# Second attention's column norms: factors spread by products, or written to DRAM and read back to all partitions

## The chip, the core and the metric

The kernel runs on one core of a Trainium2 chip. The metric is the device time of one execution in microseconds (us); the time of a kernel is the median of its runs. A profile of one execution lies beside it, taken by the hardware profiler. Times inside it are counted from the start of its span.

The engines are TensorE (PE; its weight loads are listed as PEld), VectorE (DVE), ScalarE (ACT), GpSimd (POOL) and SyncE (SP). In this kernel SP issues all transfers between DRAM and the on-chip memory (SBUF). PE writes its results to eight banks of PSUM, which are named `ps`.

## The reference, cut to what matters

The whole program is two transformer blocks in sequence. The change lies in the second one, in its second attention (stick breaking, 8 heads of 128). Ahead of that attention the queries and the keys are normed, each head's column of 128 numbers by itself:

```python
def rmsnorm(x, gain):
    xf = x.astype(jnp.float32)
    y = xf * lax.rsqrt(jnp.mean(xf * xf, axis=-1, keepdims=True) + RMS_EPS)
    return (y * gain.astype(jnp.float32)).astype(x.dtype)
...
    qs = rmsnorm(heads(sq, SB_DH), sbq_gain)
    ks = rmsnorm(heads(sk, SB_DH), sbk_gain)
    o_sb = stick_breaking_attention(qs, ks, heads(sv, SB_DH)).astype(hn.dtype).reshape(B, T, SB_W)
```

There are 528 positions, 16 learned ones and 512 of the sequence. For a query of head h at position t the factor is one over the root of the mean of 128 squares plus a small number.

## The kernel before, in words

The kernel keeps activations transposed: features lie on the 128 partitions, positions along the free dimension. A tile of one head's queries is 128 x 512, of its keys 128 x 528. So a norm needs, for each position, a sum over partitions, and then the factor of that position on all 128 partitions.

The dense products take their weights from one stream in DRAM, in chunks of 512 KB. A chunk is loaded to `raw` (L259, on SP), split into a high and a low part by ACT (`split_hi`, L272) and DVE (`split_lo`, L279), and used by 8 groups of three matmuls (`three`, L294 to L296) for each range of columns. The split of a chunk is made three chunks ahead, and it is the work of the evacuation of the chunk that has just been multiplied.

A stage is a set of lanes that run `together` (L679): each lane gives each engine a generator which yields due times, and `weave` (L667) writes the instructions of one engine in the order of those due times. An engine runs its instructions strictly in that order, waits included. At the end of the stage all engines meet.

The stage of the change, from about 1632 to 1715 us, has four lanes:

- `SecondBranch` (L1734): eight chunks of the second branch product. PE multiplies `o_hi` and `o_lo` with a chunk into bank 6 or 7; DVE evacuates it with two instructions (L1766, L1768) into `merged`, then splits the low part of a later chunk (L279); SP loads the two tiles of `branch_in` that DVE needs (L1752) and stores `merged` to DRAM (`pre_spill`, L1756). A chunk's bank is free for the chunk after next when L1766 is done. Its due times run from 0 to 8, one unit for each chunk.
- The column norms, `NormCols` (L1050), of 16 tiles: 8 of keys (`sb_k`), then 8 of queries (`v_rows`). Due times are 0.6 to 8, with a step of 0.2 for spreading. They have two passes.
- `ValueRows` (L1697): eight times a load of a value tile (L1710), five transposing products on PE (L1722, L1723), and two copies on ACT, from 5 to 8. SP's loads of it stand in one queue with those of `SecondBranch`.
- `Lead` (L789): after everything else, PE multiplies the first chunk of the next stage, so that it has work while the other engines finish.

The first pass of `NormCols` loads a tile (L1079), squares it on ACT into one half of `sq` (L1088), and adds it up over partitions with a product on PE (L1101) which puts the sums of tile i on row i of a PSUM bank, columns 0 to 263 on rows 0 to 15 and the others on rows 32 to 47. When all 16 tiles are in, ACT takes the roots (L1091), DVE the reciprocals (L1120), and DVE multiplies with a constant by row (L1121). Then `rt`, 64 x 264, holds all factors, one row for each half of a tile.

The second pass spreads the factors and norms the tiles. For tile i, PE multiplies row i of `rt` with a broadcast column of the identity (L1111), for each half; each half is recorded as two matmuls. This puts the factor of each position on all partitions of a PSUM bank. Two pairs of banks, (2, 3) and (4, 5), take turns. DVE multiplies the tile with the spread factors and with the gain of its partition, in place, one instruction for each half (L1128). PE waits with tile i until tile i-2 is normed.

The due times put the second pass of this stage between 4.8 and 8. On DVE that gives this order: one norm, the evacuation of chunk 4, five norms, chunk 5, five norms, chunk 6, five norms, chunk 7. `NormCols` is used in two more stages, which the change leaves alone. POOL has no work in this stage.

```python
    def spread_time(self, i):
        n = len(self.tiles)
        return self.t1 - (n - i) * self.step
```

Of the kernel before, what the change touches and what calls it, by code (L numbers as in the profile page):

```python
# [20 lines left out]
F32 = mybir.dt.float32  # L21
F32R = mybir.dt.float32r
ACT = mybir.ActivationFunctionType
ALU = mybir.AluOpType
# [3 lines left out]
P = 128  # L28
# [6 lines left out]
HALF = T2 // 2  # L35
# [97 lines left out]
def param_array(v):  # L133
# [12 lines left out]
    def pairs(pe):  # L146
        return pe.reshape(CMP_J, P).T
# [90 lines left out]
class Chain:  # L238


    def __init__(self, sem):
        self.sem, self.count = sem, 0
# [69 lines left out]
def cst(K, name, rows=P):  # L312

    a, n = CONST_COLS[name]
    a1 = CONST_COLS["of block 1"][0]
    return K.const1[0:rows, a - a1:a - a1 + n] if a >= a1 else K.const[0:rows, a:a + n]


def par(K, name, rows=P):
    a, n = PARAM_COLS[name]  # L320
    return K.param[0:rows, a:a + n]
# [319 lines left out]
class Lane:  # L641
# [9 lines left out]
    def pe(self, pe):  # L651
        yield from ()
# [4 lines left out]
    def dve(self, dve):  # L657
        yield from ()

    def pool(self, pool):  # L660
        yield from ()
# [17 lines left out]
def together(K, *lanes):  # L679
    with K.nc.Block() as block:  # L680
        @block.sync
        def _(sp):
            weave(sp, [lane.sp for lane in lanes])

        @block.tensor
        def _(pe):
            weave(pe, [lane.pe for lane in lanes])

        @block.scalar
        def _(act):  # L690
            weave(act, [lane.act for lane in lanes])

        @block.vector
        def _(dve):
            weave(dve, [lane.dve for lane in lanes])

        @block.gpsimd
        def _(pool):
            weave(pool, [lane.pool for lane in lanes])
# [13 lines left out]
PRODUCT_SEMS = ("banks_free", "pieces")  # L713
# [333 lines left out]
NORM_COL_SEMS = tuple(f"tile_in_{i}" for i in range(16)) + ("n_squares", "n_sums", "n_roots", "n_factors", "n_spread", "n_normed")  # L1047


class NormCols(Lane):  # L1050
# [39 lines left out]
        act.wait_ge(z["n_sums"], n)  # L1090
        act.activation(self.rt[:], K.ps[0:64, 0, 0:HALF], ACT.Sqrt, bias=self.bias).then_inc(z["n_roots"], 1)  # L1091

    def pe(self, pe):
        K, z, n = self.K, self.z, len(self.tiles)
        for i, (x, _) in enumerate(self.tiles):
            yield self.square_time(i + 0.7)
            if i == 0 and self.free is not None:
                pe.wait_ge(*self.free)
            pe.wait_ge(z["n_squares"], i + 1)
            for h, (a, e) in enumerate(self.halves(x)):  # L1100
                mm = pe.matmul(K.ps[32 * h:32 * h + 32, 0, 0:e - a], cst(K, "pick")[:, 15 - i:47 - i], self.sq[:, i % 2, a:e],  # L1101
                               start=i == 0, stop=i == n - 1, skip_group_check=True)
            mm.then_inc(z["n_sums"], 1)
        for i, (x, _) in enumerate(self.tiles):
            yield self.spread_time(i)
            if i == 0:
                pe.wait_ge(z["n_factors"], 1)
            if i >= len(self.pairs):
                pe.wait_ge(z["n_normed"], i - len(self.pairs) + 1)
            for h, (a, e) in enumerate(self.halves(x)):  # L1110
                mm = pe.matmul(K.ps[:, self.pairs[i % len(self.pairs)] + h, 0:e - a],  # L1111
                               cst(K, "ident")[32 * h:32 * h + 32, 32 * h + i:32 * h + i + 1].broadcast_to([32, P]),
                               self.rt[32 * h:32 * h + 32, 0:e - a], start=True, stop=True)
            mm.then_inc(z["n_spread"], 1)

    def dve(self, dve):
        K, z, n = self.K, self.z, len(self.tiles)
        yield self.spread_time(0) - self.step
        dve.wait_ge(z["n_roots"], 1)
        K.dve_chain.link(dve, dve.reciprocal(self.rt[:], self.rt[:]))  # L1120
        dve.tensor_scalar(self.rt[:], self.rt[:], cst(K, self.scales, 64), None, ALU.mult).then_inc(z["n_factors"], 1)  # L1121
        for i, (x, gain) in enumerate(self.tiles):
            yield self.spread_time(i + 0.5)
            dve.wait_ge(z["n_spread"], i + 1)
            by = 1.0 if gain is None else gain
            b = self.pairs[i % len(self.pairs)]
            for h, (a, e) in enumerate(self.halves(x)):
                last = dve.scalar_tensor_tensor(x[:, a:e], K.ps[:, b + h, 0:e - a], by, x[:, a:e], ALU.mult, ALU.mult)  # L1128
            last.then_inc(z["n_normed"], 1)


ROW_SEMS = ("rows_in", "r_transposed", "r_act", "r_dve")
# [561 lines left out]
VALUE_SEMS = ("values_in_0", "values_in_1", "v_t", "v_out")  # L1694
# [1262 lines left out]
def named_sems(K, *groups):  # L2957
    names = [n for g in groups for n in g]
    return dict(zip(names, sems(K, *names)))


def block2(K, v):
# [3 lines left out]
    STORED = STORED_SEMS  # L2966
    taps = par(K, "conv2").rearrange("p (g f t) -> p g f t", g=2, t=4)
    with ExitStack() as c:
# [6 lines left out]
        with ExitStack() as c2:  # L2975
# [3 lines left out]
            with ExitStack() as c3:  # L2979
# [3 lines left out]
                z = named_sems(K, PRODUCT_SEMS, ("gate_free", "gate_pieces", "convolved", "silu", "tapped", "last_square"), FACTOR_SEMS, STORED, GATE_SEMS, NORM_COL_SEMS,  # L2983
                               ROW_SEMS)
# [12 lines left out]
            z = named_sems(K, PRODUCT_SEMS, STORED, DELTA_SEMS)  # L2997
# [3 lines left out]
        with ExitStack() as c2:  # L3001
            S.qk = scratch(K, c2, "qk_cols", [P, 8, T2])
            with ExitStack() as c3:
                ring = scratch(K, c3, "ring", [P, 3, T2])
                z = named_sems(K, PRODUCT_SEMS, STORED, OUT_SEMS, NORM_COL_SEMS)
# [7 lines left out]
            with ExitStack() as c3:  # L3013
                vT = scratch(K, c3, "v_cols", [P, 8, T2])
                ring = scratch(K, c3, "ring", [P, 3, T2])
                z = named_sems(K, PRODUCT_SEMS, STORED, ROW_SEMS)
# [4 lines left out]
            z = named_sems(K, PRODUCT_SEMS, STORED, DELTA_SEMS)  # L3021
# [3 lines left out]
        with ExitStack() as c2:  # L3025
            ring = scratch(K, c2, "ring", [P, 3, T2])
            z = named_sems(K, PRODUCT_SEMS, STORED, OUT_SEMS)
            together(K, DeltaOutput(K, S, o_hi, o_lo, D2["dz"], 8, z, c2, 0, 8),
                     Stored(K, [(8, XQ, D2["gdn"], 0, rs, (ACT.Tanh, 0.5))], ring, (6, 7), z, 0, 8, 1))
        qT = S.v.rearrange("p m j n -> p (m j n)").rearrange("p (h t) -> p h t", h=8)  # L3030
        with ExitStack() as c2:
            kT, v_rows = scratch(K, c2, "sb_k", [P, SB_H, T2]), scratch(K, c2, "sb_v", [P, 5, 1024])
            with ExitStack() as c3:
                z = named_sems(K, PRODUCT_SEMS, STORED, NORM_COL_SEMS, VALUE_SEMS, ("branch_in_0", "branch_in_1", "branch_taken"))
                dense = SecondBranch(K, o_hi, o_lo, D2["br0"], D2["gdn"], D2["pre"], c3, (6, 7), z, 0, 8)
                together(K, NormCols(K, [(kT[:, i], par(K, "sbk_gain")) for i in range(8)] + [(qT[:, i], par(K, "sbq_gain")) for i in range(8)],
                                     [(D2["sbk"], i) for i in range(8)] + [(D2["sbq"], i) for i in range(8)], None, 128 * EPS,
                                     "sb_scales", (2, 4), z, c3, 0.6, 8, 0.2),
                         ValueRows(K, v_rows, D2["sbv"], z, c3, 0, (z["n_roots"], 1), 5, 8),
                         dense, Lead(K, XQ, dense))  # L3040
            with ExitStack() as c3:
                ring = scratch(K, c3, "ring", [P, 2, SEQ])
                z = named_sems(K, PRODUCT_SEMS, STORED, STICK_SEMS)
                together(K, StickBreaking(K, qT, kT, v_rows, z, c3, 0, 8),
                         Stored(K, [(8, XQ, D2["gsb"], 0, rs, None)], ring, (6, 7), z, 0, 8, 1))
# [6 lines left out]
def core_setup(nc, ctx, v, n_stream):  # L3052
    K = Core()
    K.live, K.cleared, K.uid = [], [], 0
    K.nc, K.stage, K.at, K.stream, K.n_stream = nc, 0, 0, v["stream"], n_stream

    def sb(name, shape, dt=F32):
        return ctx.enter_context(nc.sbuf_tensor(name, shape, dt))

    K.ps = ctx.enter_context(nc.psum_tensor("ps", [P, 8, 512], F32))  # L3060
    K.raw = sb("raw", [P, RAW, 1024])
    K.whi, K.wlo = sb("whi", [P, HL, 1024], F32R), sb("wlo", [P, HL, 1024], F32R)
    K.h = sb("h_sb", [P, KT, SEQ])
    K.const, K.param = sb("const_sb", [P, CONST_COLS["of block 1"][0]]), sb("param_sb", [P, PARAM_N])
    K.nx_hi, K.nx_lo = sb("nx_hi", [P, KT, T2], F32R), sb("nx_lo", [P, KT, T2], F32R)
    K.spill = {n: nc.dram_tensor(f"{n}_spill", (P, w, T2), F32, kind="Internal").ap() for n, w in (
        ("qk0", 8), ("v0", 8), ("qk1", 8), ("v1", 8), ("dz", 16), ("sbq", 8), ("sbk", 8), ("sbv", 8), ("br0", 8), ("gdn", 8),
        ("pre", 8), ("gsb", 8))}
    K.s_out = ctx.enter_context(nc.semaphore("out_written"))
    K.t_ss, K.t_rs = sb("t_ss", [P, TT]), sb("t_rs", [P, TT])  # L3070
    K.s_raw = [ctx.enter_context(nc.semaphore(f"raw_in_{i}")) for i in range(RAW)]
    K.s_hi, K.s_lo, K.s_used = [ctx.enter_context(nc.semaphore(n)) for n in ("hi_made", "lo_made", "chunk_used")]
    K.act_chain = Chain(ctx.enter_context(nc.semaphore("act_step")))
    K.dve_chain = Chain(ctx.enter_context(nc.semaphore("dve_step")))
    K.pool_chain = Chain(ctx.enter_context(nc.semaphore("pool_step")))
    return K
# [39 lines left out]
```

## Time and profile before

| | us |
|---|---|
| median of 3 runs (2331.86 to 2341.15) | 2336.89 |
| the profiled execution's own time | 2338.18 |
| its span | 2336.4 |
| busy PE | 2225.7 |
| busy DVE | 1125.4 |
| busy ACT | 813.3 |
| busy POOL | 64.6 |

The profiled execution is 1.3 us above the median, and 1.8 us of its time lie outside the span. The profile's busy time of an engine is an average over stages with different limits; the stage of the change is a small part of the span, and which engine bounds it has to be read from that stretch. The chain of work that ended last can be followed back only through the last 18% of the span, so it says nothing of this stage.

### The profile page before, as it was taken

Reading aid. Unit: us, or ns where it says so; the run is one execution under the profiler, and the core shown is the slowest. Engines: PE = TensorE matmul, PEld = TensorE weight load, DVE = VectorE, ACT = ScalarE, POOL = GpSimd, SP = SyncE. Lnnn points to the kernel's source line nnn. Section 1 sums busy time; section 2 is a strip of 40 time slices with the busy share of each in tenths; the row PEclk is TensorE's granted clock in tenths of the full one; section 3 lists DMA queues with packets and bytes.
Section 4 is the critical chain, followed back from the end, with each engine's and each line's share of the span. In section 5 each row is a group of like instructions: output and inputs, shape, how many; then the busy total and the mean of one; then the engine's idle time right before and its main releaser. Section 6 shows DMA issues by size and latency. Waiting matters only on the chain. (4 is left out here: it accounts for less than half of the span.)

```text
span 2336.4 us, 32788 instructions
## 1 busy us (share of the span) xinstructions
PE 2225.7 (95%) x13572; PEld 1706.8 (73%) x13572; DVE 1125.4 (48%) x1804; ACT 813.3 (35%) x1326; POOL 64.6 (3%) x88
## 2 busy tenths in 40 slices
PE   8999799999999899989998999998999999999999
PEld 7776457777778898976765788766565578888887
DVE  3465675666643366654434534345432245444422
ACT  3342554333332443332214222225355533322211
POOL 0000001000000000000000000000011101000000
PEclk9999799999999999999999999999999999999999
DMA  4124001222232243321114322114721132222222
GB/s 165 65 72 144 1 1 63 90 82 90 81 108 90 78 151 120 122 103 65 61 67 152 123 95 69 56 59 159 239 73 41 56 143 90 96 93 97 92 97 90
DMA packets 78595, 218.62 MB, mean 94 GB/s; under 512 B 8688, under 2 KB 13168, under 8 KB 78448
## 3 DMA queue, kind: packets, MB, share of 16 engines
q1 hardware_dynamic: 78448, 216.54, 26.7%
q8 instruction: 107, 1.75, 0.3%
q14 instruction: 40, 0.33, 0.0%
HBM read 185.70 MB, written 29.75 MB: 92 GB/s over the span
## 5 line engine op out<-in xcount | busy, mean ns | idle before, releaser
L294 PE MATMUL ps<-nx_hi,whi 128*128 128x264 f32 (+1 forms) x1504 | 543.0, 361 | 17.4 <-DVE nx_lo L383 9.9
L279 DVE TENSOR_TENSOR wlo<-raw,whi 128x1024 fp32r<-128x1024 f32 x282 | 346.5, 1229 | 393.4 <-ACT whi L272 392.9
L295 PE MATMUL ps<-nx_lo,whi 128*128 128x264 f32 (+1 forms) x1504 | 515.0, 342 | 0.0
L296 PE MATMUL ps<-nx_hi,wlo 128*128 128x264 f32 (+1 forms) x1504 | 514.7, 342 | 0.0
L272 ACT ACTIVATE whi<-raw 128x1024 fp32r<-128x1024 f32 x282 | 297.8, 1057 | 524.5 <-PE ps L296 422.7
L294 PEld LDWEIGHTS ps<-nx_hi,whi 128*128 128x128 f32 x1504 | 288.9, 192 | 82.4 <-issue 34.5
L296 PEld LDWEIGHTS ps<-nx_hi,wlo 128*128 128x128 f32 x1504 | 289.2, 192 | 32.8
L295 PEld LDWEIGHTS ps<-nx_lo,whi 128*128 128x128 f32 x1504 | 289.8, 193 | 29.3 <-issue 1.7
L294 PE MATMUL ps<-x_hi,whi 128*128 128x512 f32 x528 | 209.8, 397 | 14.8 <-DVE wlo L279 14.8
L296 PE MATMUL ps<-x_hi,wlo 128*128 128x512 f32 x528 | 209.8, 397 | 0.0
L295 PE MATMUL ps<-x_lo,whi 128*128 128x512 f32 x528 | 208.4, 395 | 0.0
L294 PEld LDWEIGHTS ps<-x_hi,whi 128*128 128x128 f32 x528 | 99.1, 188 | 45.5 <-DVE wlo L279 22.7
L295 PEld LDWEIGHTS ps<-x_lo,whi 128*128 128x128 f32 x528 | 99.2, 188 | 24.2
L296 PEld LDWEIGHTS ps<-x_hi,wlo 128*128 128x128 f32 x528 | 99.1, 188 | 23.1
L294 PE MATMUL ps<-act_hi,whi 128*128 128x512 f32 x288 | 113.3, 393 | 0.9 <-DVE wlo L279 0.9
L296 PE MATMUL ps<-act_hi,wlo 128*128 128x512 f32 x288 | 114.1, 396 | 0.0
L295 PE MATMUL ps<-act_lo,whi 128*128 128x512 f32 x288 | 114.0, 396 | 0.0
L294 PE MATMUL ps<-o_hi,whi 128*128 128x512 f32 x192 | 84.5, 440 | 8.7 <-DVE o_lo L1922 4.5
L858 DVE TENSOR_TENSOR ring<-ps,factor 128x512 f32<-128x512 f32 (+1 forms) x72 | 41.2, 572 | 82.8 <-PE ps L296 78.4
L295 PE MATMUL ps<-o_lo,whi 128*128 128x512 f32 x192 | 77.3, 402 | 0.0
L296 PE MATMUL ps<-o_hi,wlo 128*128 128x512 f32 x192 | 76.7, 399 | 0.0
L593 DVE TENSOR_TENSOR ps<-ps,factor 128x512 f32<-128x512 f32 x66 | 45.8, 693 | 49.7 <-PE ps L296 49.7
(454 smaller groups left out, 2906.9 us busy)
## 6 DMA issues: line engine op xcount, KB each, us to landing
raw<-stream_dram SPq DMA_DIRECT2D x285, 512.0 KB, 3.5
qk_spill<-ring SPq DMA_DIRECT2D x16, 264.0 KB, 2.2
qk_cols<-qk_spill SPq DMA_DIRECT2D x16, 264.0 KB, 4.0
v_spill<-ring SPq DMA_DIRECT2D x16, 264.0 KB, 2.1
v_cols<-v_spill SPq DMA_DIRECT2D x16, 264.0 KB, 4.2
dz_spill<-ring SPq DMA_DIRECT2D x16, 256.0 KB, 2.1
dz<-dz_spill SPq DMA_DIRECT2D x16, 256.0 KB, 5.1
sbk_spill<-ring SPq DMA_DIRECT2D x8, 264.0 KB, 2.1
```

The lines of the kernel that those rows point to most:

```text
L272: act.activation(K.whi[:, n % HL], K.raw[:, n % RAW], ACT.Copy).then_inc(K.s_hi, 1)
L279: dve.tensor_tensor(K.wlo[:, n % HL], K.raw[:, n % RAW], K.whi[:, n % HL].bitcast(F32), ALU.subtract).then_inc(K.s_lo, 1)
L294: pe.matmul(out, whi, xhi, start=start, stop=False, skip_group_check=skip)
L295: pe.matmul(out, whi, xlo, start=False, stop=False, skip_group_check=skip)
L296: return pe.matmul(out, wlo, xhi, start=False, stop=stop, skip_group_check=skip)
L593: dve.tensor_tensor(ps, ps, rs[:], ALU.mult).then_inc(z["scaled"], 1)
L858: dve.tensor_tensor(y, ps, by[:, a:e], ALU.mult).then_inc(self.free, 1)
```

## The change

The column norms of this stage become `NormColsByRow`. The first pass and the factors in `rt` stay. In the second pass PE has no work any more. POOL writes `rt` to a new DRAM tensor of 64 x 264, waits until it has landed, and then reads, for each half of each tile, the one row of factors into all 128 partitions of `sq`, whose two halves (free after the first pass) take turns. POOL waits with tile i until tile i-2 is normed. DVE norms a tile from `sq` in one instruction for its whole width instead of two. Due times on DVE are as before.

```diff
+class NormColsByRow(NormCols):
...
+    def pool(self, pool):
+        z = self.z
+        pool.wait_ge(z["n_factors"], 1)
+        pool.dma_start(self.factors, self.rt[:]).then_inc(z["factors_out"], 16)
+        pool.wait_ge(z["factors_out"], 16)
+        for i, (x, _) in enumerate(self.tiles):
+            if i >= 2:
+                pool.wait_ge(z["n_normed"], i - 1)
+            for h, (a, e) in enumerate(self.halves(x)):
+                pool.dma_start(self.sq[:, i % 2, a:e],
+                               self.factors[32 * h + i:32 * h + i + 1, 0:e - a].broadcast_to([P, e - a])).then_inc(z[f"spread_in_{i % 2}"], 16)
+        yield from ()
+
+    def pe(self, pe):
+        yield from self.sums(pe)
+
+    def dve(self, dve):
+        z = self.z
+        yield from self.roots(dve)
+        for i, (x, gain) in enumerate(self.tiles):
+            yield self.spread_time(i + 0.5)
+            dve.wait_ge(z[f"spread_in_{i % 2}"], 32 * (i // 2 + 1))
+            n = x.shape[1]
+            dve.scalar_tensor_tensor(x[:, 0:n], self.sq[:, i % 2, 0:n], 1.0 if gain is None else gain, x[:, 0:n],
+                                     ALU.mult, ALU.mult).then_inc(z["n_normed"], 1)
...
-                together(K, NormCols(K, [(kT[:, i], par(K, "sbk_gain")) for i in range(8)] + [(qT[:, i], par(K, "sbq_gain")) for i in range(8)],
+                together(K, NormColsByRow(K, K.factors, [(kT[:, i], par(K, "sbk_gain")) for i in range(8)] + [(qT[:, i], par(K, "sbq_gain")) for i in range(8)],
...
+    K.factors = nc.dram_tensor("factors_spill", (64, HALF), F32, kind="Internal").ap()
```

`sums` and `roots` are the first halves of `pe` and `dve` of `NormCols`, cut out as functions without a change to what they issue.

## Rows read from the trace of the kernel before

**Rows 1.** The page, part 1: busy time, share of the span, instructions of each engine.
```profile
PE 2225.7 (95%) x13572; PEld 1706.8 (73%) x13572; DVE 1125.4 (48%) x1804; ACT 813.3 (35%) x1326; POOL 64.6 (3%) x88
```

**Rows 2.** Busy time by stretch of the stage; at the end granted clock, DMA share, GB/s.
```profile
1674.00:1687.00 13.00, 13.00 (x69) 7.87 (x68) 7.70 (x15) 3.29 (x7) 0.00 (x0) 1.00 0.62 208
...
1698.40:1709.20 10.80, 10.80 (x56) 6.84 (x57) 6.75 (x14) 3.21 (x8) 0.00 (x0) 1.00 0.16 52
```

**Rows 3.** Waits from 1633 to 1715: us in total, times, the longest.
```profile
DVE merged L1766 <- PE ps L296: 30.6, 5, 11.1
```

**Rows 4.** Timeline of PE: start, duration of one, what; the last two at the stage's end.
```profile
1673.47 0.39 PE L295 MATMUL ps<-o_lo,whi 128*128 128x512 f32 x1
1673.71 0.40 PE L296 MATMUL ps<-o_hi,wlo 128*128 128x512 f32 x1
1674.03 0.71 PE L1111 MATMUL ps<-rt,const_sb 32*128 32x264 f32 x4
...
1675.02 0.39 PE L295 MATMUL ps<-o_lo,whi 128*128 128x512 f32 x1
...
1714.33 0.40 PE L296 MATMUL ps<-nx_hi,wlo 128*128 128x512 f32 x1
1715.05 0.46 PE L1802 MATMUL ps<-v_rows,sb_k 128*128 128x128 f32 x2 [0.32 <-PEq L680]
```

**Rows 5.** Timeline of DVE in the stage.
```profile
1673.41 0.35 DVE L1121 TENSOR_SCALAR rt<-rt,const_sb 64x264 f32<-64x264 f32 x1
1674.80 0.89 DVE L1128 SCALAR_TENSOR_TENSOR sb_k<-ps,param_sb,sb_k 128x264 f32<-128x264 f32 x2 [1.04 <-PE ps L1111]
1675.68 0.69 DVE L1766 SCALAR_TENSOR_TENSOR merged<-ps,branch_in 128x512 f32<-128x512 f32 x1
...
1678.15 1.82 DVE L1128 SCALAR_TENSOR_TENSOR sb_k<-ps,param_sb,sb_k 128x264 f32<-128x264 f32 x4
...
1708.28 0.88 DVE L1128 SCALAR_TENSOR_TENSOR v_rows<-ps,param_sb,v_rows 128x264 f32<-128x264 f32 x2 [1.86 <-PE ps L1111]
```

**Rows 6.** Line 927, the same DVE operation of 528 columns from SBUF: ns least/median/most.
```profile
L927 DVE SCALAR_TENSOR_TENSOR ring<-z,param_sb,ring x32: 768/769/771, 801.8 to 1029.8; 128x528 f32<-128x528 f32 x32
```

**Rows 7.** Issues on SP by line: ns least/median/most; below L2592 its us to landing.
```profile
L1710 SPq DMA_DIRECT2D v_cols<-sbv_spill x8: 319/320/457, 1669.5 to 1697.7; - x8
...
L1752 SPq DMA_DIRECT2D branch_in<-gdn_spill x8: 424/432/1331, 1632.5 to 1694.7; - x8
...
L2592 SPq DMA_DIRECT2D rows<-cols x4: 522/594/600, 193.6 to 197.4; - x4
...
DMA to landing us min/median/max: 2.3/2.3/2.3
```

**Rows 8.** Groups of POOL by form: busy us, mean ns of one.
```profile
L563 POOL TENSOR_TENSOR up<-up,gate 128x512 f32<-128x512 f32 x20 | 28.3, 1414 | 853.2 <-ACT gate L514 853.2
...
L1900 POOL TENSOR_TENSOR later_sum<-later_sum,softplus 128x384 f32<-128x384 f32 x8 | 8.0, 1005 | 0.0
```

**Rows 9.** DMA issues from 1633 to 1716: KB each, median us from issue to landing.
```profile
v_cols<-sbv_spill SPq DMA_DIRECT2D x8, 264.0 KB, 2.8
pre_spill<-merged SPq DMA_DIRECT2D x8, 256.0 KB, 2.0
...
branch_in<-gdn_spill SPq DMA_DIRECT2D x7, 256.0 KB, 5.8
```

**Rows 10.** Timeline of PE at a later stage's start, after an idle time.
```profile
1915.65 0.63 PE L294 MATMUL ps<-nx_hi,whi 128*128 128x512 f32 x1 [4.30 <-PEq L680]
1916.08 0.63 PE L295 MATMUL ps<-nx_lo,whi 128*128 128x512 f32 x1
```

**Rows 11.** Busy time by stretch, there: the last three are granted clock, DMA share, GB/s.
```profile
1915.60:1919.40 3.80, 3.75 (x10) 2.95 (x11) 0.00 (x0) 0.00 (x0) 0.00 (x0) 0.55 0.70 262
```

**Rows 12.** Timeline of POOL: its first two-input operation.
```profile
372.43 1.86 POOL L563 TENSOR_TENSOR up<-up,gate 128x512 f32<-128x512 f32 x1 [371.99 <-ACT gate L514]
```

More of the change, by code:

```diff
@@ L1091, in act, with sums @@
         act.activation(self.rt[:], K.ps[0:64, 0, 0:HALF], ACT.Sqrt, bias=self.bias).then_inc(z["n_roots"], 1)
-    def pe(self, pe):
+    def sums(self, pe):
         K, z, n = self.K, self.z, len(self.tiles)
@@ L1103, in pe @@
             mm.then_inc(z["n_sums"], 1)
+    def pe(self, pe):
+        K, z = self.K, self.z
+        yield from self.sums(pe)
         for i, (x, _) in enumerate(self.tiles):
@@ L1114, in pe, with roots @@
             mm.then_inc(z["n_spread"], 1)
-    def dve(self, dve):
-        K, z, n = self.K, self.z, len(self.tiles)
+    def roots(self, dve):
+        K, z = self.K, self.z
         yield self.spread_time(0) - self.step
@@ L1121, in dve @@
         dve.tensor_scalar(self.rt[:], self.rt[:], cst(K, self.scales, 64), None, ALU.mult).then_inc(z["n_factors"], 1)
+    def dve(self, dve):
+        K, z = self.K, self.z
+        yield from self.roots(dve)
         for i, (x, gain) in enumerate(self.tiles):
@@ L1129, in dve, with __init__, pe @@
             last.then_inc(z["n_normed"], 1)
+class NormColsByRow(NormCols):
+    def __init__(self, K, factors, *args, **kw):
+        super().__init__(K, *args, **kw)
+        self.factors = factors
+    def pool(self, pool):
[10 more added lines that the diff above has]
+        yield from ()
+    def pe(self, pe):
+        yield from self.sums(pe)
+    def dve(self, dve):
+        z = self.z
+        yield from self.roots(dve)
+        for i, (x, gain) in enumerate(self.tiles):
[4 more added lines that the diff above has]
+                                     ALU.mult, ALU.mult).then_inc(z["n_normed"], 1)
 ROW_SEMS = ("rows_in", "r_transposed", "r_act", "r_dve")
@@ L3033, in block2 @@
             with ExitStack() as c3:
-                z = named_sems(K, PRODUCT_SEMS, STORED, NORM_COL_SEMS, VALUE_SEMS, ("branch_in_0", "branch_in_1", "branch_taken"))
+                z = named_sems(K, PRODUCT_SEMS, STORED, NORM_COL_SEMS, VALUE_SEMS, ("factors_out", "spread_in_0", "spread_in_1", "branch_in_0", "branch_in_1", "branch_taken"))
                 dense = SecondBranch(K, o_hi, o_lo, D2["br0"], D2["gdn"], D2["pre"], c3, (6, 7), z, 0, 8)
-                together(K, NormCols(K, [(kT[:, i], par(K, "sbk_gain")) for i in range(8)] + [(qT[:, i], par(K, "sbq_gain")) for i in range(8)],
+                together(K, NormColsByRow(K, K.factors, [(kT[:, i], par(K, "sbk_gain")) for i in range(8)] + [(qT[:, i], par(K, "sbq_gain")) for i in range(8)],
                                      [(D2["sbk"], i) for i in range(8)] + [(D2["sbq"], i) for i in range(8)], None, 128 * EPS,
```

## The prediction

> **What bounds the kernel now.** The page first: TensorE (PE) is busy 95% of the span [rows 1], so a change that takes work off PE can pay only where PE's own work ends the stage. Next the stretches of the stage from 1674 us, where the spreading products begin, to 1715 us, where the stage ends [rows 2]: in the two stretches shown PE is busy without a gap, while VectorE (DVE) is busy some 60% and the DMA engines 62% early and 16% late. The waits of the stage say the same from the other side: DVE waits 30.6 us for PE's finished products [rows 3]. The end is PE's too: its last product, of the next stage's leading chunk, starts at 1714.33, and the next stage's first matmul at 1715.05 [rows 4], 0.3 us after it ends.
>
> **What is removed.** Sixteen spreading steps on PE, four recorded matmuls each. Around the first one the second term of a product starts at 1673.47 and the next second term at 1675.02 [rows 4]; without a spreading step these three matmul places take 3 x 0.233 us, the pitch between 1673.47 and 1673.71 being 0.24. A step therefore costs 1.55 - 0.70 = 0.85 us of PE, and sixteen cost 13.6 us, all on the path. If nothing else became late, PE would be done at 1714.7 - 13.6 = 1701.1.
>
> **What is added.** One write of 64 rows and 32 reads, two for each tile, all on POOL's queue. In this stage POOL has nothing else, so no work is queued behind them. The reads fill the two halves of sq in turn: the reads of tile i wait until tile i-2 is normed. So there is a loop: norm of i, two issues on POOL, landing, norm of i+2. Two tiles go round in one such loop. With g for an issue on POOL, L from the end of an issue to landing and n for the norm on DVE, a loop takes 2g + L + n.
>
> n: before, a norm is two instructions, four of them 1.82 us [rows 5], so 0.91 a tile. After, it is one instruction of 528 columns from SBUF; the same operation in that form takes 0.77 us [rows 6]. I take 0.77. DVE gains a little, and DVE is not the bound.
>
> g: no DMA is issued by POOL in this trace. Lower end 0.32 us, the shortest issue by SP in this stage [rows 7]; upper end 1.41 us, POOL's longest operation on 128 partitions [rows 8]. It is POOL that has to do it, for 128 rows and both sides of the transfer, so the row that it is nearest to is one of POOL's own between its short and long ones, the 128x384 sum at 1.005 us. I take 1.0.
>
> L: lower end 1.7 us: an issue of 128 KB between tiles lands 2.3 us after its start, of which the issue is 0.6 [rows 7]. Upper end 5.4 us: in this stage the last load of each burst that SP issues, branch_in, lands in 5.8 us [rows 9], of which 0.43 is issue [rows 7]. The 264 KB loads of v_cols in the same stage land in 2.8 us, of which 0.32 is issue, so 2.5 for twice the bytes of a read. I take 2.3.
>
> **The schedule that follows.** The factors are ready at 1673.41 + 0.35 = 1673.8 [rows 5]. The write: issue 1.0, and 2.0 to land, as a store of this stage does [rows 9]: 1676.8. POOL then issues four reads: tile 0 lands at 1676.8 + 2.0 + 2.3 = 1681.1, tile 1 at 1683.1. The first norm ends at 1681.9, where the first one of before started at 1674.8.
>
> DVE runs its instructions in a fixed order: norm 0, evacuation of chunk 4, norms 1 to 5, evacuation of chunk 5, norms 6 to 10, chunk 6, norms 11 to 15, chunk 7. An evacuation is 2.47 us, from 1675.68 to 1678.15 [rows 5]. Put through this order, with POOL taking the pairs of issues one after the other, norm 1 ends at 1685.2, norm 5 at 1695.4, norm 10 at 1708.9 and norm 15 at 1722.4. The loop is 2.0 + 2.3 + 0.77 = 5.07 us, 2.5 us a tile, against 36.8 us for sixteen tiles before (1674.8 to about 1709.2, 2.15 a tile, PE's pace). Queued behind the waiting norms on DVE are the evacuations of chunks 4 to 7; behind those, on SP, the stores of the merged tiles and the value and weight loads that follow a store; and on PE the products that need a bank. They come late, but PE still ends its leading chunk at about 1715, ahead of DVE.
>
> After norm 15 the last evacuation has 1.4 us until its second instruction ends, then the store takes 2.0 to land and SP waits for it: 1722.4 + 1.4 + 2.1 = 1725.9. With the 0.3 us that the boundary takes now, the next stage starts at 1726.2, 11.2 us later than now.
>
> One cost follows: PE then idles for some 10 us. After an idle of 4.30 us matmuls start 0.43 apart instead of 0.23 [rows 10], and the granted clock is 0.55 on average over the 3.8 us up to 1919.4, so for nearly all of them it is the lower level (1.2 GHz) [rows 11]: 10 matmuls are recorded there, and eight pitches with 0.20 extra make 1.6 us. I take 1.7. **Sum: 11.2 + 1.7 = +12.9 us.** The profiled execution is 2338.18 us, 1.3 above the median of the runs (2336.89); it would become 2351.1, the median 2349.8. I say 2350.
>
> The sum moves by 7.5 us for each microsecond of 2g + L. It crosses zero near 2g + L = 2.8 and reaches 0.5% (11.7 us, about what a measurement of this kernel can tell from no change) near 4.1, with the clock's cost.
>
> One-off start: POOL's first two-input operation takes 1.86 us [rows 12] against a mean of 1.41 for its form [rows 8], so 0.5 us for a first use, which I leave out as small. The Trainium skill (GPSIMD Engine Reference, section Instruction dispatch) has the first call of a freshly loaded GpSimd routine pay about 6 us for loading code; by that rule, if it held for the first DMA issued here, the sum would be some +19 instead of +12.9. The row above shows less than a tenth of it, for another routine.
>
> **The rivals.**
>
> *Cheap reads (0.22), not slower.* If POOL issues as SP does (0.32) and a read lands in the quiet 1.7, the loop is 2 x 0.32 + 1.7 + 0.77 = 3.1 us, norm 15 ends at 1707.9 and the stage at 1711.7: -3.3 us, 2333.6. With L = 2.3 it is +0.9, 2338. For it: the low DMA share late in the stage. Against it: no row shows POOL doing anything on 128 partitions and hundreds of elements as fast as SP issues. It decides at 2g + L below 2.8. The Trainium skill (DMA: Bandwidth & Descriptors, section Anatomy of one DMA) gives a GpSimd-issued DMA about 2.0 us plus its bytes over 436 GB/s, an estimate of 2.3 us from issue to landing; with g = 1.0 that would be L = 1.3 and a sum of +4 to +6.
>
> *Nothing becomes late (0.04), faster.* All 13.6 us come back: 2323.3. It needs reads that keep PE's new pace of 2.15 - 0.85 = 1.3 us a tile, so 2g + L + 0.77 of at most 2.6; the lowest ends of both give 3.1.
>
> *Slow landing (0.28), slower.* The reads share the engines with SP's bursts, and all 128 partitions fetch the same row of DRAM. If each pair lands as branch_in does (L = 5.4), the loop is 8.2 us and the stage ends 34.3 us later: 2372.9 with the clock. With g = 1.41 as well, +43. Against it: the reads have a queue of their own, and the engines are 84% idle late in the stage [rows 2].
>
> The forecast itself (0.46) covers g from 0.7 to 1.4 at L of 1.7 to 2.5, from +5 to +20.
>
> **How the numbers follow.** The range goes from cheap reads, 2333, to the slow landing with a little of the dearer issue, 2376; outside it are the full gain and the dearest corner. Faster by over 0.5% is the full gain alone, 0.04. Within 0.5%: cheap reads (0.22) and under half of the forecast's spread (0.19), 0.41. Slower: the rest of the forecast (0.27) and the slow landing (0.28), 0.55.
>
> **What would show it.** Right: the first norm near 1682, norms in pairs about 5 us apart, DVE's waits on DMA into sq where it waited for PE; about 1 us between POOL's issues; PE idle some 10 us ahead of the next stage and slow for its first 4 us. Wrong: norms closer than 2.1 us a tile (then PE or SP ends the stage and the time falls), or reads that land over 4 us after issue (then far slower). If PE is still busy up to the boundary, the reading that DVE's chain ends the stage is wrong.

## The result, and the profile after

| | us |
|---|---|
| median after, 4 runs (2351.55 to 2356.86) | 2354.86 |
| median before, 4 runs (2331.86 to 2341.15) | 2334.88 |
| ratio after to before, with its 95% interval | 1.0075 [1.005, 1.0099] |
| the profiled execution after: own time, span | 2353.14, 2351.3 |

The changed kernel is 20 us slower by the medians (the interval is 12 to 23 us), where +12.9 was forecast (2350, range 2333 to 2376). The two profiled executions differ by only 14.9 us, because the one after happens to reach the stage 5.6 us earlier than the one before. Such scatter lies mostly ahead of the stage: in the profiled executions of the kernels before and after and of the eight versions in B to E, the factors are ready between 1665.1 and 1675.3 us, while what follows the stage takes 621.4 to 623.8 us in all ten. So the stage is compared by itself: from the end of the instruction that makes the factors to the first matmul of the next stage. Before that is 1673.41 + 0.35 to 1715.05 [rows 4, 5], 41.3 us. After it is 1668.21 to 1728.03, 59.8 us: +18.5.

On the page of the kernel after, part 1 has less PE and more POOL than [rows 1], and part 3 has a queue that was not there, the one that POOL's transfers use (1568 packets, 4.33 MB). The lines are from those two parts:

```profile
PE 2213.7 (94%) x13508; PEld 1703.8 (72%) x13508; DVE 1121.4 (48%) x1788; ACT 814.0 (35%) x1326; POOL 83.7 (4%) x121
...
q0 software_dynamic: 1568, 4.33, 1.1%
```

The same two stretches as [rows 2] look quite different (columns as there). PE, which was busy all the time at a clock of 1.00, is busy 3.80 of 13 us in the first one, and the DMA engines are 82% busy late in the stage where they were at 16%:

```profile
1674.00:1687.00 13.00, 3.80 (x13) 2.81 (x12) 4.64 (x6) 0.75 (x2) 3.25 (x6) 0.67 0.78 208
1698.40:1709.20 10.80, 9.03 (x36) 7.39 (x37) 3.31 (x5) 2.86 (x6) 3.25 (x6) 0.68 0.82 267
```

The waits from 1674 us on (us in total, times, the longest). DVE waits 36.6 us for the reads, in 14 waits; in the same stretch of the kernel before it waited 13.4 us for the spreading products. (The 30.6 us of [rows 3] are another matter: 30.1 of them lie ahead of the factors, and the kernel after has them too, 30.0.) PE waits for the value tiles and then for the end of the stage:

```profile
DVE sb_k L1170 <- DMA sq<-factors_spill: 20.5, 6, 7.9
...
DVE v_rows L1170 <- DMA sq<-factors_spill: 16.1, 8, 3.4
...
PE ps L1764 <- DMA v_cols<-sbv_spill: 15.2, 2, 9.2
...
PE ps L1844 <- PEq L680: 11.6, 1, 11.6
```

POOL's view of the reads (ns least/median/most of an issue; below, us from issue to landing, the write included) and its timeline at the start. An issue costs 0.55 us, the first one of all 0.71; the four first reads go out in one go, and from then on POOL waits for a norm before each pair:

```profile
L1156 POOL DMA_DIRECT2D sq<-factors_spill x32: 546/546/571, 1671.4 to 1719.4; - x32
L1150 POOL DMA_DIRECT2D factors_spill<-rt x1: 712/712/712, 1668.5 to 1668.5; - x1
...
DMA to landing us min/median/max: 2.6/4.0/6.1
```

```profile
1668.53 0.71 POOL L1150 DMA_DIRECT2D factors_spill<-rt  x1 [134.97 <-DVE rt L1125]
1671.45 2.18 POOL L1156 DMA_DIRECT2D sq<-factors_spill  x4 [2.21 <-DMA factors_spill<-rt]
1677.18 1.08 POOL L1156 DMA_DIRECT2D sq<-factors_spill  x2 [3.55 <-DVE sb_k L1170]
1680.32 1.08 POOL L1156 DMA_DIRECT2D sq<-factors_spill  x2 [2.06 <-DVE sb_k L1170]
```

DVE's timeline answers to [rows 5]. A norm takes 0.77 us, and in front of nearly each one DVE sits idle for `sq`:

```profile
1667.86 0.35 DVE L1125 TENSOR_SCALAR rt<-rt,const_sb 64x264 f32<-64x264 f32 x1
1676.12 0.77 DVE L1170 SCALAR_TENSOR_TENSOR sb_k<-sq,param_sb,sb_k 128x528 f32<-128x528 f32 x1 [7.90 <-DMA sq<-factors_spill]
...
1682.44 0.77 DVE L1170 SCALAR_TENSOR_TENSOR sb_k<-sq,param_sb,sb_k 128x528 f32<-128x528 f32 x1 [2.42 <-DMA sq<-factors_spill]
1687.03 0.77 DVE L1170 SCALAR_TENSOR_TENSOR sb_k<-sq,param_sb,sb_k 128x528 f32<-128x528 f32 x1 [3.82 <-DMA sq<-factors_spill]
...
1692.42 0.77 DVE L1170 SCALAR_TENSOR_TENSOR sb_k<-sq,param_sb,sb_k 128x528 f32<-128x528 f32 x1 [2.43 <-DMA sq<-factors_spill]
...
1723.41 0.75 DVE L1170 SCALAR_TENSOR_TENSOR v_rows<-sq,param_sb,v_rows 128x512 f32<-128x512 f32 x1 [1.89 <-DMA sq<-factors_spill]
```

PE's timeline: an idle for a value tile inside the stage, and the boundary, which answers to the last of [rows 4]:

```profile
1683.75 1.12 PE L1764 MATMUL ps<-const_sb,v_cols 128*128 128x128 f32 x4 [9.20 <-DMA v_cols<-sbv_spill]
...
1728.03 0.77 PE L1844 MATMUL ps<-v_rows,sb_k 128*128 128x128 f32 x2 [11.57 <-PEq L680]
```

Last, the transfers of the stage (1660 to 1740 us), KB each and us to landing. Everything that shares the engines with the reads lands later than in [rows 9]: `v_cols` 5.0 instead of 2.8, `branch_in` 7.8 instead of 5.8, the store 4.8 instead of 2.0. The packets of the reads' queue took 32.3% of the 16 engines' time in these 80 us, 25.8 us:

```profile
q0 software_dynamic: 1568, 4.33, 32.3%
...
sq<-factors_spill POOLq DMA_DIRECT2D x24, 132.0 KB, 4.0
v_cols<-sbv_spill SPq DMA_DIRECT2D x8, 264.0 KB, 5.0
...
pre_spill<-merged SPq DMA_DIRECT2D x5, 256.0 KB, 4.8
...
branch_in<-gdn_spill SPq DMA_DIRECT2D x3, 256.0 KB, 7.8
```

In the same 80 us of the kernel before, the same transfers (no queue of POOL's exists there):

```profile
v_cols<-sbv_spill SPq DMA_DIRECT2D x8, 264.0 KB, 2.8
pre_spill<-merged SPq DMA_DIRECT2D x6, 256.0 KB, 2.0
...
branch_in<-gdn_spill SPq DMA_DIRECT2D x4, 256.0 KB, 4.9
```

**How the pieces hang together.** A norm waits for its two reads; the evacuation of a chunk stands behind the norms on DVE; SP's store waits for the evacuation; and the loads of `v_cols` stand behind the store on SP. PE then waits for `v_cols`. For the first wait the times show it: the evacuation of chunk 4 starts 8.6 us behind the factors (1676.80), where it was 1.9 [rows 5], and SP's timeline goes on

```profile
1678.24 0.32 SPq L1798 DMA_DIRECT2D pre_spill<-merged  x1
1678.60 0.93 SPq L1752 DMA_DIRECT2D v_cols<-sbv_spill  x2
```

So PE's 9.2 us at 1683.75 are mostly the reads' lateness, passed on through three queues; about 2 us of them are the slower landing of `v_cols` itself.

### The profile page after: what moved, and what is told of

Read it like the earlier page. It is cut to its first block and busy times, and to the rows that moved or that the text cites. A ratio compares the mean times of both kernels' runs of the same rounds, so it can differ in the third digit from the quotient of the medians.

```text
span 2351.3 us, 32680 instructions
## 1 busy us (share of the span) xinstructions
PE 2213.7 (94%) x13508; PEld 1703.8 (72%) x13508; DVE 1121.4 (48%) x1788; ACT 814.0 (35%) x1326; POOL 83.7 (4%) x121
## 3 DMA queue, kind: packets, MB, share of 16 engines
q0 software_dynamic: 1568, 4.33, 1.1%
## 5 line engine op out<-in xcount | busy, mean ns | idle before, releaser
L294 PE MATMUL ps<-x_hi,whi 128*128 128x512 f32 x528 | 209.9, 398 | 14.9 <-DVE wlo L279 14.9
```

What stands on the lines that cost most here:

```text
L294: pe.matmul(out, whi, xhi, start=start, stop=False, skip_group_check=skip)
```

## The experiments

The question: why does a loop take longer than in the forecast? From the first norm to the sixteenth it is 1676.12 to 1723.41, 47.3 us for 15 steps, so 6.3 us for two tiles. The forecast's own schedule, with the evacuations in it, has 40.5 us and 5.4. Two things were suspected in the landing: that 128 partitions fetch one and the same row of DRAM, and that the reads share the engines with SP's bursts. Also open were the price of an issue and the depth of the buffers. Each ratio is to the kernel before on the same chip.

**A. The disputed transfer by itself.** The second attention is as before (norms by products). In an earlier stage, around 267 to 421 us, POOL and after it SP issue reads of 132 KB, pairs of them, and 264 KB, four times each, and wait for each to land: "same" fetches one row for all partitions, "rows" 128 different rows.

```diff
+                            src = w[3:4, 0:m].broadcast_to([P, m]) if a == "same" else w[:, 0:m]
+                            eng.dma_start(probes[a, k][:, h * HALF:h * HALF + m], src).then_inc(sem, 16)
```

> The kernel before, with 32 reads issued by POOL and then 32 by SP in the first block's attention, a stretch with almost no other transfers; nobody waits for them but their issuer, so the time should stay that of the kernel before. In the changed kernel a read's issue takes 0.55 us and it lands 4.0 us (median) after its start. Hot row (one DRAM row fetched for all 128 partitions is slow): reads of one row land at least 1 us later than reads of 128 different rows, from POOL and from SP alike. Slow POOL path: POOL's reads land at least 1 us later than SP's, whichever the source. Shared engines (SP's bursts in the stage make them late): all kinds land in 2 to 2.6 us here, with little between them.

Four single reads of each kind by POOL, then by SP (issue, ns; below each, us to landing):

```profile
L2806 POOL DMA_DIRECT2D same_one__43<-stream_dram x4: 536/620/709, 267.0 to 277.8; - x4
DMA to landing us min/median/max: 3.1/3.4/3.7
...
L2806 POOL DMA_DIRECT2D rows_one__46<-stream_dram x4: 536/536/536, 313.6 to 321.7; - x4
DMA to landing us min/median/max: 2.3/2.5/2.5
...
L2806 SPq DMA_DIRECT2D same_one__43<-stream_dram x4: 328/328/328, 352.1 to 360.7; - x4
DMA to landing us min/median/max: 2.9/2.9/3.1
...
L2806 SPq DMA_DIRECT2D rows_one__46<-stream_dram x4: 328/328/328, 390.3 to 396.8; - x4
DMA to landing us min/median/max: 2.0/2.1/2.3
```

One row for all partitions costs 0.9 us more than 128 rows by POOL and 0.8 by SP, in a stretch with few other transfers; at least 1 us was expected. POOL's issue of the same read takes 0.21 us more than SP's, and its landing, counted from the start of the issue, 0.4 to 0.5 us more, not the 1 us that a slow path of POOL's was to cost. The run took 2394.4 us, one time only: SP's own reads, from 352 on, delayed its next load of weights to 421.12, and PE waited 59.8 us for the end of the stage. That this would cost no time was wrong, but it does not touch the durations.

**B. One row or many, with and without SP's bytes.** Three runs complete a table of two by two with the kernel after. In the first the reads fetch 128 different rows of the weight stream instead of the factors, so the norms multiply with other numbers; all else is the same.

```diff
-                pool.dma_start(self.sq[:, i % 2, a:e],
-                               self.factors[32 * h + i:32 * h + i + 1, 0:e - a].broadcast_to([P, e - a])).then_inc(z[f"spread_in_{i % 2}"], 16)
+                pool.dma_start(self.sq[:, i % 2, a:e], self.K.stream[2 * i + h][:, 0:e - a]).then_inc(z[f"spread_in_{i % 2}"], 16)
```

> The changed kernel, but each read fetches 128 different rows of the weight stream instead of one row of factors 128 times; the norms are made with these numbers, so the spreading is left out. Same bytes, same issues. Hot row: the landing falls from 4.0 to about 2.5 us, a loop of two tiles from 5.4 to 3.9, and the time by some 11 us, to about 2344. Slow POOL path or shared engines: the landing stays near 4 and the time within 3 us of 2355.

In the second the reads are those of the kernel after, and SP's later loads of this stage (value tiles from the third on, weights and `branch_in` from chunk 5 on) carry 16 columns each, so later products work on old data. The third does both.

```diff
-            sp.dma_start(self.vT[:, f % 2], self.src[:, f]).then_inc(self.z[f"values_in_{f % 2}"], 16)
+            m = 16 if f >= 2 else T2
+            sp.dma_start(self.vT[:, f % 2, 0:m], self.src[:, f, 0:m]).then_inc(self.z[f"values_in_{f % 2}"], 16)
...
```

> The changed kernel, but from chunk 5 on SP's loads in the stage (weights, branch_in, value tiles) fetch 16 columns instead of whole tiles, so the bursts beside the reads are gone; stale data is used in their place. Alone, a pair of reads of one row took 4.0 to 4.3 us from the first issue to the next pair's; with the norm that is a loop of about 5 us instead of 6.3 (3.15 a tile measured). If SP's bursts make the reads late, the time falls by some 7 us, to 2346 to 2350. If the hot row alone does it, it stays within 3 us of 2355.

> Both: 128 different rows as the source, and SP's loads cut to 16 columns from chunk 5 on. Alone such a pair took 3.3 us, so the loop is 4.2 us, 2.1 a tile, what PE needed with its products. If hot row and bursts together are all of the landing that the forecast lacks, the time is 2338 to 2343, near the kernel before; if POOL's path or something else adds more, it stays above 2346.

| reads | SP's bytes | stage, us | POOL's pair issued to norm, mean us | read lands, median us | median, us | ratio to before |
|---|---|---|---|---|---|---|
| one row (after) | full | 59.8 | 5.3 | 4.0 | 2354.86 | 1.0075 [1.005, 1.0099] |
| many rows | full | 53.4 | 4.6 | 2.6 | 2352.75 | 1.0074 [1.005, 1.0098] |
| one row | few | 55.1 | 4.5 | 3.8 | 2347.47 | 1.006 [1.004, 1.0081] |
| many rows | few | 45.7 | 3.3 | 2.5 | 2344.49 | 1.0031 [1.0014, 1.0048] |

The fourth column runs from the start of a pair of issues to the start of its norm, over the 12 or 13 norms from the third on for which DVE waited for the reads. Against the kernel after, many rows take 6.4 us off the stage, few bytes 4.7, and both 14.1, more than the sum of 11.1. These are stages of one profiled execution each. In the whole time neither step alone stands out against the kernel after: their intervals overlap, and for many rows, where some 11 us were expected, the ratio is almost the same. Both together do (1.0031 [1.0014, 1.0048] against 1.0075 [1.005, 1.0099]). So it is shown that the one row and the bursts together make most of the lateness; what each is worth alone, and that each makes the other worse, rests on the stages. Both together were expected to reach 2338 to 2343; they reached 2344.49.

How the one row and the many differ on the engines is seen in the share of POOL's queue, in an 80 us stretch around the stage, for the same 1568 packets and 4.33 MB: 32.3% with one row, in the kernel after and with few bytes alike, and with many rows and full bytes

```profile
q0 software_dynamic: 1568, 4.33, 17.0%
```

The packets took 25.8 us of all engines against 13.6. This is no fixed price of one row, though. The same reads took 20.2 us with the four buffers of D, and the longer reads of C 17.3; in the stretch of A, four reads of 132 KB by POOL took 2.8 us of all engines (one row) and 1.7 (many), but four of 264 KB 4.0 and 3.8, and SP's four of 132 KB 1.8 and 1.9, though they land 0.8 us apart. What the bursts do is seen in the many-rows run, where a norm right behind a burst of SP's waits long and its neighbours hardly (DVE's timeline):

```profile
1686.14 0.77 DVE L1169 SCALAR_TENSOR_TENSOR sb_k<-sq,param_sb,sb_k 128x528 f32<-128x528 f32 x1 [0.76 <-DMA sq<-stream_dram]
1693.08 0.77 DVE L1169 SCALAR_TENSOR_TENSOR sb_k<-sq,param_sb,sb_k 128x528 f32<-128x528 f32 x1 [6.17 <-DMA sq<-stream_dram]
1694.12 0.77 DVE L1169 SCALAR_TENSOR_TENSOR sb_k<-sq,param_sb,sb_k 128x528 f32<-128x528 f32 x1 [0.27 <-DMA sq<-stream_dram]
```

In that run SP issued the weights and `branch_in` from 1684.97 on.

**C. Fewer issues.** The factors are laid out so that a tile has one row of 528, and each tile takes one read of 264 KB instead of two.

```diff
+            pool.dma_start(self.sq[:, i % 2, 0:n], self.factors[i:i + 1, 0:n].broadcast_to([P, n])).then_inc(z[f"spread_in_{i % 2}"], 16)
```

> The changed kernel, with the factors laid out as 16 rows of 528 in DRAM and one read for each tile instead of two (16 issues instead of 32, the same bytes). If the loop norm, issues, landing, norm sets the end, one issue of 0.55 us leaves it, eight loops follow each other, and the time falls by 4 to 5 us, to 2350. If the time of a transfer grows with its bytes (hot row), the landing grows and the gain is under 3 us. If something else sets the end, no change.

2348.43 us, ratio 1.0062 [1.0041, 1.0083]; the stage takes 55.5 us and a read lands in 3.8. Sixteen issues of 0.54 us less (and the write in two parts) take 4.3 us off the stage, a small part of the 18.5. The longer reads also took less of the engines, 17.3 us instead of 25.8, so not all of the 4.3 need be the issues.

**D. Deeper buffers.** `sq` gets two more buffers, so POOL may run four tiles ahead of the norms instead of two.

```diff
-            if i >= 2:
-                pool.wait_ge(z["n_normed"], i - 1)
+            if i >= 4:
+                pool.wait_ge(z["n_normed"], i - 3)
```

> The changed kernel with four buffers for the spread factors instead of two, so four tiles are under way. If the latency of the loop sets the end, a tile takes (1.09 + 3.5 + 0.77)/4 = 1.3 us and POOL's issues or the transfers (about 0.8 us of all engines for each read, 1.6 a tile) become the bound: the stage shortens by some 15 us, to 2335 to 2342. If the transfers' own rate set it already (2.7 us a tile), no change, 2355.

2345.85 us over 10 runs, ratio 1.0036 [1.0017, 1.0054], where 2335 to 2342 were expected. The stage takes 48.3 us, 11.5 less than after, so the loop makes most of what the kernel after lost. But the end is now PE's (it waits 0.32 us at the boundary, as before), and PE has waited for value tiles:

```profile
1681.54 1.12 PE L1768 MATMUL ps<-const_sb,v_cols 128*128 128x128 f32 x4 [9.33 <-DMA v_cols<-sbv_spill]
1692.10 1.11 PE L1768 MATMUL ps<-const_sb,v_cols 128*128 128x128 f32 x4 [3.71 <-DMA v_cols<-sbv_spill]
...
1714.17 0.46 PE L1848 MATMUL ps<-v_rows,sb_k 128*128 128x128 f32 x2 [0.32 <-PEq L680]
```

The waits are 14.7 us, and PE also runs slower: the granted clock over the stage is 0.82 instead of 1.00, and PE is busy for 32.8 us where its 41.0 of before, without the spreading, would be 28. Waits and clock are more than what PE was spared, so the stage is 7 us longer than before.

Do the loads come late because they stand behind a store that waits for an evacuation behind the norms? The next version gives the norms due times of 5.05 + 0.18 i, so that DVE takes the evacuations earlier.

```diff
-            yield self.spread_time(i + 0.5)
+            yield 5.05 + 0.18 * i
```

> Four buffers, and the norms' due times on DVE moved so that the evacuation of chunk 4 stands ahead of norm 0 and six norms ahead of that of chunk 5. In the run with four buffers the end was PE's, 7 us late, and PE had stood still for value tiles whose loads SP had queued behind the store of chunk 4. If that queueing is what is left, the time falls by 3 to 6 us from 2346, to 2340 to 2343. If the reads' rate is, it stays at 2346 or rises.

2345.99 us, ratio 1.004 [1.0022, 1.0057]: nothing gained (the stage takes 47.1 us). PE still waits 14.0 us for `v_cols`, in four waits (1.21, 6.12, 5.35, 1.36), and the median landing of `v_cols` from 1665 to 1725 is 6.3 us. The first wait, 9.33 us before, is down to 1.21, but later ones have grown. The order on DVE was not the cause that was left; the transfers that share the engines with the reads are late themselves.

**E. Only a part by reads.** Tiles 0 to 7 by products as before, 8 to 15 by reads into four buffers; then the same with only the last four tiles by reads, all issued right behind the write.

```diff
+    BY_PRODUCT = 8
...
+        for i, (x, _) in list(enumerate(self.tiles))[self.BY_PRODUCT:]:
+            if i >= self.BY_PRODUCT + 4:
+                pool.wait_ge(z["n_normed"], i - 3)
```

> The keys' eight tiles by products as before, the queries' eight by reads into four buffers, started as soon as the factors have landed. PE is spared 8 x 0.85 = 6.8 us, and the first reads have some 17 us to land. If the reads' start and rate are hidden behind the keys' tiles, 2331 to 2334, faster than both; if PE still waits for DVE or SP, 2336 to 2342.

2339.24 us over 12 runs against 2337.99, ratio 1.0 [0.9983, 1.0017]. The stage takes 44.0 us. PE is spared 6.8 us of products by the forecast's 0.85 a tile and waits 5.6 us for `v_cols` (1.36, 0.77 and 3.48); its granted clock from 1690 to 1709 is 0.86 instead of 1.00, so it gives back more than it was spared, and the stage is 2.7 us longer than before.

> Tiles 0 to 11 by products, as in the kernel of before; only the last 4 tiles (12 to 15) by reads, into four buffers of their own, so POOL issues all 8 reads right behind the write, with no wait for a norm. PE is spared 4 x 0.85 = 3.4 us. Theory (what eats the gain of the eight-tile mix is that the reads' traffic delays SP's loads while PE needs them, 5.6 us of waits for v_cols): with half of the traffic, over by about 1690, PE waits under 1.5 us for v_cols after 1690, the stage (factors ready to the next stage's first matmul) takes 38.5 to 40.5 us against 41.3, and the time is 1 to 3 us below the kernel of before. Rival (a burst of loads that is once late stays late, however short the reads are): PE still waits 3 us or more, the stage takes 41 to 44 us and no time is gained.

2337.53 us over 12 runs against 2339.11, ratio 0.9993 [0.9977, 1.0009]. The stage takes 38.1 us, 3.2 less than before: PE is spared four steps and has no wait for a tile. The four norms of the last tiles run without a pause, though their reads took 4.0 to 8.3 us, since they were issued 20 us ahead. The views are POOL's reads into the first of the two pairs of buffers, DVE's timeline, and PE's three stretches:

```profile
L1161 POOL DMA_DIRECT2D sq<-factors_spill x4: 546/546/571, 1678.2 to 1679.8; - x4
```

```profile
1702.25 1.41 DVE L1182 SCALAR_TENSOR_TENSOR v_rows<-sq,param_sb,v_rows 128x512 f32<-128x512 f32 x2
1703.57 1.41 DVE L1182 SCALAR_TENSOR_TENSOR v_rows<-spread,param_sb,v_rows 128x512 f32<-128x512 f32 x2
```

```profile
1674.00:1690.00 16.00, 16.00 (x83) 9.85 (x82) 10.41 (x19) 4.62 (x9) 5.04 (x9) 1.00 0.82 231
1690.00:1705.00 15.00, 15.00 (x79) 10.06 (x78) 10.48 (x20) 4.24 (x11) 0.00 (x0) 1.00 0.55 183
1705.00:1713.00 8.00, 7.68 (x36) 6.02 (x35) 2.52 (x3) 1.88 (x4) 0.00 (x0) 1.00 0.09 33
```

This is the expected mechanism, and in the stage slightly more than the expected size (38.5 to 40.5); in the whole time a gain of 0.1% is inside the interval. No version was shown to be faster than the kernel before.

## Why the prediction was right, and where its terms were not

The sign, the shape and the range held: DVE's norms, fed by POOL's loop, end the stage in PE's place, and PE idles and starts the next stage slowly. That the number came as near as it did is partly luck, as the terms show. Point by point, in us after the factors are ready (forecast from its schedule, with 1673.8 as zero; measured with 1668.21):

| end of | forecast | measured |
|---|---|---|
| norm 0 | 8.1 | 8.7 |
| norm 1 | 11.4 | 11.8 |
| norm 5 | 21.6 | 25.0 |
| norm 10 | 35.1 | 40.7 |
| norm 15 | 48.6 | 56.0 |
| stage (next first matmul) | 52.4 | 59.8 |

- **Removed: right.** Four tiles fewer took 3.2 us off a stage that PE ends, 0.81 us a tile, against 0.85 forecast.
- **Start: right.** The write and the first reads together were 0.6 us off.
- **n: right.** 0.77 us.
- **g: mis-sized.** "I take 1.0"; measured 0.546, nearer to SP's issue than to POOL's arithmetic, the row it was taken from.
- **L: mis-sized the other way.** "I take 2.3"; a pair's data is there 5.3 us after its first issue starts, so L is 5.3 - 2 x 0.55 = 4.2. The read of different rows in A would have given 2.5 - 0.55 = 2.0, near the value taken; one row and the bursts made the rest. Of the text's signs of being wrong, reads that land over 4 us after issue, the median read (4.1) is on the edge.
- **2g + L**, the term of the sum, was 5.3 instead of 4.3. With the forecast's own 7.5 us per us this is +7.5, and the stage missed by 59.8 - 52.4 = 7.4. The two errors had opposite signs, so the forecast was nearer than its reasons deserved: the measured pair of terms lies outside what it said it covers (g from 0.7 to 1.4, L from 1.7 to 2.5). The close match is itself partly luck, since the loop of the text lacks a step: from the end of a norm to POOL's next issue 0.29 us pass (1676.89 to 1677.18). Put through the schedule of the text, the measured g and L give some 6.5 us more, with this step 8.2 (an estimate). The four runs of B lie on the same line to within some 2 us: from 5.3 to 3.3 it would give -15, measured -14.1.
- **Behind norm 15: right.** 1.4 + 2.1 + 0.3 = 3.8 forecast; 1724.16 to 1728.03 is 3.9.
- **The clock: right.** PE idled 11.57 us, then in the stretch below the granted clock is 0.50, the lower level. Forecast +1.7.

```profile
1728.00:1732.00 4.00, 3.97 (x12) 3.21 (x13) 0.44 (x2) 3.38 (x7) 0.29 (x1) 0.50 0.38 131
```

  The same product of the attention on PE's timeline, after and then before, starts 1737.32 - 1728.03 = 9.29 us behind the stage's first matmul and 1722.60 - 1715.05 = 7.55 [rows 4]: +1.74.

```profile
1737.32 0.38 PE L1844 MATMUL ps<-v_rows,sb_k 128*128 128x128 f32 x2
```

```profile
1722.60 0.39 PE L1802 MATMUL ps<-v_rows,sb_k 128*128 128x128 f32 x2
```

Stage and clock make 18.5 + 1.7 = 20.2, where the medians are 20.0 apart and the interval is 12 to 23.

- **PE ahead of DVE by some 10 us: right (11.57) by luck.** The text has PE done at about 1715, 41 us behind the factors; it was done at 1716.46, 48.3 behind them, so PE was as late as DVE. The text says that PE's products come late, but works out no wait for it. PE waited 15.2 us for `v_cols`, more than the 13.6 us spared, and was busy for 33.0 us where its 41.0 of before without the spreading would be 28: behind its 9.2 us of idle, products start 0.43 us apart (1685.73, 1686.16) instead of 0.23. So the missing price was not only the loop: the reads slow the loads that PE lives on. With deep buffers, where PE ends the stage again, the wait is still 14.7 us, and the stage is 7 us longer than before.
- **Two readings off, without weight in the sum.** The 30.6 us that DVE waits for PE belong almost wholly to the stretch ahead of the factors; that PE bounded the stage behind them rests on the stretches of [rows 2]. And the "36.8 us for sixteen tiles" are 34.4 by the text's own two times.
- **Rivals.** Nothing late: refuted. Cheap reads: its issue was half right (0.55), its landing wrong; even many rows with few bytes stayed 4.4 us of stage above before, at 3.3 where the text had the zero at 2.8. Slow landing: its two reasons, the one row and the shared engines, are what the runs showed, at L of 4.2 instead of 5.4.
- **The pages.** The estimate from the Trainium skill (DMA: Bandwidth & Descriptors, section Anatomy of one DMA), 2.3 us from issue to landing, agrees with the read of many rows in A (2.5) and not with one row (3.4) or with the stage (4.0); the +4 to +6 that it gave is refuted. The 6 us that the Trainium skill (GPSIMD Engine Reference, section Instruction dispatch) gives for the first call of a freshly loaded routine were not seen at the first issue: it took 0.71 us against 0.546. The Trainium skill (DMA: Bandwidth & Descriptors, section Issuing engines are not separate DMA queues) says that transfers of all issuers run on the same engines. The trace agrees (`v_cols` 2.8 to 5.0). The prediction weighed this sharing for the reads, in its rival of a slow landing, but not for the loads beside them; and "the reads have a queue of their own", put forward against that rival, was no defence.

Still open: why one row lands later than many, and why its packets take longer in POOL's short reads alone. The runs show that it is so, not in which part of the memory or the engines it arises.

## What to carry to other kernels

Before work is moved from a busy engine to transfers, price a transfer as it will run: with its source pattern, among the bursts of its stage, and with what it does to the loads that the busy engine itself waits for. A loop of two buffers around a transfer runs at its latency, not at its bandwidth; the reads that were issued 20 us early cost no wait here. When a forecast comes out near, still check its terms one by one: here one was too high by 0.45 us and the other too low by 1.9.

## What was not expected of the hardware

- Reading one row of DRAM into 128 partitions took 3.4 us by POOL and 2.9 by SP where 128 rows of the same length took 2.5 and 2.1. In the stage its packets took 25.8 us of all engines instead of 13.6 for 4.33 MB; for POOL's reads of twice the length and for SP's reads, in A, the two took nearly the same.
- The two causes of a slow landing were worth 6.4 and 4.7 us of stage alone and 14.1 together, by one profiled execution of each.
- POOL issued a transfer of 128 rows in 0.55 us, about half of its 128x384 sum (1.005) [rows 8], which the forecast had taken as nearest.
